# Sparse attention of a two-layer decoder step: scores and values as split fp32r products, a denser compression, probabilities scaled on GpSimd

## The reference, cut to what matters

```python
def compress(k, pe, w):                    # stride 16, blocks of 32 tokens
    ...
    blocks = jnp.concatenate([seg[:, i:i + nc] for i in range(r)], axis=2)
    return jnp.einsum('nclgd,lde->ncge', blocks + pe[:, None, :], w)

def nsa_core(q, q_rot, qpos, ck, cv, fetch, wk, wv, wpos, gates, key_len):
    ...
    p_cmp = jnp.where(cvalid, jax.nn.softmax(jnp.where(cvalid, s, NEG_INF), axis=-1), 0.0)
    o_cmp = jnp.einsum('bghqn,bngd->bqghd', p_cmp.astype(cv.dtype), cv)
    ...
    o = gates[..., 0:1] * o_cmp + gates[..., 1:2] * o_slc + gates[..., 2:3] * o_win
```

## Time and profile before

| what | us |
|---|---|
| runs | 1518.56, 1520.88, 1523.13 |
| median of the runs | 1520.88 |
| profiled execution, span of the core | 1521.6 |
| PE busy | 1469.1 (97%) |
| DVE, POOL, ACT busy | 577.0, 515.6, 484.7 |

### The profile page before, as it was taken

The page is one execution under the profiler, slowest core; times in us unless marked ns, Lnnn a source line. Parts: engine busy times, 40 slices in busy tenths (PEclk is TensorE's granted clock), DMA queues, the critical chain, the costliest instruction groups (busy, mean ns, idle before and its releaser), DMA issues.

```text
span 1521.6 us, 26668 instructions
## 1 busy us (share of the span) xinstructions
PE 1469.1 (97%) x10754; PEld 1322.9 (87%) x10754; DVE 577.0 (38%) x985; ACT 484.7 (32%) x731; POOL 515.6 (34%) x136
## 2 busy tenths in 40 slices
PE   7997999999999999999898999999899999999998
PEld 6997999999999999999584445447799999999997
DVE  5347442222223333143556555552242222223232
ACT  5311342232232333112015556552233222223232
POOL 6422334334336555332201000000233443444652
PEclk9998999999999999999979999999899999999999
DMA  5221222332322333353610000006233223222332
GB/s 188 84 84 56 85 84 83 101 92 83 94 82 77 95 95 111 111 133 120 125 54 22 1 1 1 0 1 184 46 100 95 83 84 109 83 74 82 89 95 76
DMA packets 208062, 124.02 MB, mean 82 GB/s; under 512 B 30964, under 2 KB 205100, under 8 KB 207998
## 3 DMA queue, kind: packets, MB, share of 16 engines
q1 hardware_dynamic: 207998, 123.14, 27.6%
HBM read 117.75 MB, written 5.38 MB: 81 GB/s over the span
## 4 chain that ended last, share of the span: by engine, by line
PE 50%; issue 33%; POOL 10%; SPq 2%; DMA 2%; DVE 1%; ACT 1%; POOLq 0%; DVEq 0%; ACTq 0%
PE PG L430 31%; POOL WL L1632 10%; PE PG L974 5%; PE M L1020 5%; PE M L1008 3%; PE M L947 2%; DMA WBD<-in_w_cmp 1%; PE PG L958 1%; POOL SQX L1627 1%; DMA SLOT<-in_cache_win 1%; PE M L1120 1%; SPq L785 1%; PE M L908 1%; SPq L789 1%; SPq L790 0%
## 5 line engine op out<-in xcount | busy, mean ns | idle before, releaser
L1632 POOL TENSOR_TENSOR WL<-WR,WH 128x2048 fp32r<-128x2048 f32 x105 | 484.6, 4615 | 691.4 <-ACT WH L490 691.4
L430 PE MATMUL PG<-H,WH 128*128 128x260 f32 x4128 | 671.4, 285 | 18.7 <-DVE P L1855 11.0
L430 PEld LDWEIGHTS PG<-H,WH 128*128 128x128 f32 x4128 | 568.4, 190 | 21.3 <-DVE P L1855 11.4
L430 PE MATMUL PG<-H,WL 128*128 128x260 f32 x2064 | 417.5, 283 | 0.0
L430 PEld LDWEIGHTS PG<-H,WL 128*128 128x128 f32 x2064 | 319.7, 189 | 0.0
L430 PE MATMUL PG<-G,WH 128*128 128x260 f32 x1920 | 309.2, 283 | 1.5 <-DVE G L1392 1.5
L490 ACT ACTIVATE WH<-WR 128x2048 fp32r<-128x2048 f32 x105 | 200.4, 1908 | 275.5 <-PE PG L430 243.6
L430 PEld LDWEIGHTS PG<-G,WH 128*128 128x128 f32 x1920 | 263.7, 189 | 1.7 <-issue 1.7
L430 PE MATMUL PG<-G,WL 128*128 128x260 f32 x960 | 194.0, 283 | 0.0
L430 PEld LDWEIGHTS PG<-G,WL 128*128 128x128 f32 x960 | 148.5, 189 | 0.0
L607 DVE TENSOR_TENSOR TB<-PG,RSTD 128x520 f32<-128x520 f32 x44 | 30.8, 699 | 213.0 <-PE PG L430 213.0
(11 more groups left out here) (228 smaller groups left out, 1071.0 us busy)
## 6 DMA issues: line engine op xcount, KB each, us to landing
WR<-in_w_ffn_in SPq DMA_DIRECT2D x88, 512.0 KB, 4.6
WR<-in_w_in SPq DMA_DIRECT2D x32, 512.0 KB, 4.4
WR<-in_w_ffn_out SPq DMA_DIRECT2D x32, 384.0 KB, 3.8
WR<-in_w_ffn_out SPq DMA_DIRECT2D x32, 320.0 KB, 3.2
WR<-in_w_in SPq DMA_DIRECT2D x18, 256.0 KB, 3.5
WR<-in_w_out SPq DMA_DIRECT2D x8, 512.0 KB, 3.8
PST<-in_cache_kv SPq DMA_DIRECT2D x32, 128.0 KB, 2.1
WR<-in_w_out SPq DMA_DIRECT2D x16, 256.0 KB, 5.9
```

The lines of the kernel that those rows point to most:

```text
L430: mm = pe.matmul(PG[:, par, hf, 0:HALF], w, x, start=(first and at_k == 0 and n == 0), stop=(last and at_k == nk - 1 and n == 2))
L1632: w_split.on(pool.tensor_tensor(WL[:, b, :], WR[:, b, :], WH[:, b, :].bitcast(F32), ALU.subtract))
```

## The change

- **Compression.** `CT` holds two tokens of a pair of rows in the two partition halves, so 8 matrices `WC` (128 x 128, two half blocks side by side) replace 32 `WBD`: 8 x 2 products of 320 and 322 columns. Half of the result is then in the other partition half: ACT copies it across (`other_half`) and DVE adds (`drain_ck`). A page is loaded by four DMAs. `WC` is loaded as soon as its slot is free.
- **Queries and keys.** POOL forms the rotated queries in `RT` (cosine product, then sum), ACT writes the high part to `QST`, DVE the low part to the other partition half. Keys get a high part `KA` (ACT) and a low part `KB` (DVE), and SP copies each to the other partition half (`d_dup`). A score is then two fp32r products, and the mask.
- **Values** are split into `VSH` (ACT) and `VSL` (POOL), laid out with zeros between the halves, so that a product writes all 128 partitions. `PT` becomes `PTH` (ACT) and `PTL` (DVE); a key tile is three fp32r products.
- **The loop** runs over 88 tiles (`UNITS`). Probabilities have three buffers, scores come two steps ahead, spread over the tiles of a step (`share`); a reciprocal of four columns on DVE, scaling on POOL.
- **The compressed softmax**: subtraction and final multiplication move from DVE to POOL; the mask after the exponential goes (the maximum is cut off at NEG/10).
- **Order.** Padding of the sample queries, loads of sample keys 1 to 7, of the sample constants and of the first output weights, and the split of the first of these, move behind the loop or its last score.

```diff
+        UNITS = [(hu, kt) for hu, (gp, i, e, br) in enumerate(STEPS)
+                 for kt in ([None] if hu % 4 == 0 else []) + list(range(i + 1))]
...
+            for kv in range(2):
+                for h in range(2):
+                    for b in range(2):
+                        sp.dma_start(WC[h * HD:(h + 1) * HD, kv, :, b, :],
...
+            for n, (gp, e, br) in enumerate(STACKS):
...
+                sp.wait_ge(k_lo.sem, n + 1)
+                for x in (KA, KB):
+                    sp.dma_start(x[other, br, 2 * gp + e, :].bitcast(F32), x[r, br, 2 * gp + e, :].bitcast(F32)
+                                 ).then_inc(d_dup[n], 16)
...
+            sp.wait_ge(v_lo.sem, 1)
+            cache(0, 0, 0)
+            sp.wait_ge(s_done.sem, 4 * len(STEPS))
+            for n in range(1, NS):
                 cache(0, n, 0)
+            sp.dma_start(CS[:, :], a["c_smp"]).then_inc(d_cs, 16)
+            sp.wait_ge(pv_done.sem, len(UNITS))
             for n in range(NS):
                 cache(1, n, 0)
             for n in range(NS):
                 cache(0, n, 1)
-            sp.wait_ge(ss_done.sem, 2)
+            sp.wait_ge(d_kv, 32 * (QT + 1))
+            load_out1(sp, 0)
             for n in range(NS):
                 cache(1, n, 1)
+            load_out1(sp, 1)
...
+            for m in range(KD):
+                if m >= 3:
+                    pool.wait_ge(qst_ok.sem, m - 2)
+                x = RT[:, m % 3, :]
+                rt_cos.on(pool.tensor_tensor(x, P0[:, m, :], COS, ALU.mult))
+                pool.wait_ge(rt_cos.sem, m + 1)
+                pool.wait_ge(rope_in.sem, 4 + m + 1)
+                rt_ok.on(pool.tensor_tensor(x, x, SQ[:, m % 2, :], ALU.add))
...
+            for hu in range(len(STEPS)):
+                if hu < 2:
+                    c_ready.on(pool.tensor_tensor(TC[hu][:, :, :, :], TC[hu][:, :, :, :], spread(hu), ALU.mult))
+                gp, i, e, br = STEPS[hu]
+                pool.wait_ge(rc_ok.sem, hu + 1)
+                for j in range(4):
+                    pj = PB[hu % 3][j][:, 0:(i + 1) * P]
+                    f, g = 32 + 4 * (hu % 4) + j, 3 * (4 * (2 * gp + e) + j) + 1 + br
+                    p_ready.on(pool.tensor_scalar(pj, pj, ST4[:, f:f + 1], GT[:, i, g:g + 1], ALU.mult, ALU.mult))
+            pool.wait_ge(s_done.sem, 4 * len(STEPS))
+            z_q.on(pool.memset(QPD[:, :], 0.0))
...
-                for l in range(32):
+                for r in range(8):
...
+                    for c, n in ((0, 2 * GSEG), (1, 2 * GSEG + 2)):
+                        mm = pe.matmul(M[:, 2 + c, 0:n], WC[:, kv, r, :, :].rearrange("p b e -> p (b e)"),
+                                       CT[:, r, c * 2 * GSEG:c * 2 * GSEG + n], start=r == 0, stop=r == 7)
...
+                pe.matmul(bank[:, 0:n], q, KA[:, br, 2 * gp + e, 0:n], start=True, stop=False)
+                pe.matmul(bank[:, 0:n], q, KB[:, br, 2 * gp + e, 0:n], start=False, stop=False)
...
+                pe.matmul(O, vh, hi, start=kt is None, stop=False)
+                pe.matmul(O, vh, lo, start=False, stop=False)
+                pv_done.on(pe.matmul(O, vl, hi, start=False, stop=last))
...
+            for j in range(4):
+                score(1, j)
+            for x, (hu, kt) in enumerate(UNITS):
+                if hu + 2 < len(STEPS):
+                    for j in share(hu, x - U_0[hu]):
+                        score(hu + 2, j)
+                if x >= 2:
+                    pv(x - 2)
+                turn(x)
...
+            for m in range(KD):
+                if m >= 2:
+                    dve.wait_ge(rt_ok.sem, m - 1)
+                dve.wait_ge(rope_p.sem, 4 + m + 1)
+                rope_in.on(dve.tensor_tensor(halves(SQ[:, m % 2, :]), rope_banks(4 + m), halves(SIN), ALU.mult))
+                if m:
+                    stack_low(m - 1)
...
+            stack_low(KD - 1)
...
+            for n in range(len(STACKS)):
+                key_low(n)
+                if n == 1:
+                    dve.wait_ge(cmp_done.sem, 1)
+                    prompt_ct(dve, 1, 1, ct_v)
             for job in SETUP_V:
                 drain_job(dve, 0, job)
...
+            for x, (hu, kt) in enumerate(UNITS):
+                if hu + 2 < len(STEPS):
+                    for j in share(hu, x - U_0[hu]):
+                        row_max(hu + 2, j)
+                if x == U_0[hu] and hu + 1 < len(STEPS):
+                    recip(hu + 1)
+                low_part(x)
...
+            for x, (hu, kt) in enumerate(UNITS):
+                high_part(act, x)
...
+                if hu + 2 < len(STEPS):
+                    for j in share(hu, x - U_0[hu]):
+                        exp(hu + 2, j)
```

More of the change, by code:

```diff
@@ L344, in program @@
         d_wc = [sem("d_wc_k"), sem("d_wc_v")]
+        d_dup = [sem(f"d_dup{n}") for n in range(8)]
         d_kv, d_gs, d_cs = (sem(n) for n in ("d_kv", "d_gs", "d_cs"))
@@ L654, in program @@
         Q_ATT = Q_CV + 2
[L655 to L662, removed]
+        UNITS = [(hu, kt) for hu, (gp, i, e, br) in enumerate(STEPS)
+                 for kt in ([None] if hu % 4 == 0 else []) + list(range(i + 1))]
+        N_U = [sum(1 for h, _ in UNITS if h == hu) for hu in range(len(STEPS))]
+        U_0 = [sum(N_U[:hu]) for hu in range(len(STEPS) + 1)]
+        Q_SMP = Q_ATT + len(UNITS)
         KV_TILE = (12, 16)
         def by_act(q):
-            return Q_ATT <= q < Q_SMP or q % 2 == 1
+            return q % 2 == 1 and q != Q_CV and not Q_ATT <= q < Q_SMP
         DRAINED = [[by_act(x) for x in range(q + 1)].count(by_act(q)) for q in range(Q_SMP + 2 * NS + 4)]
@@ L1296, in pad_queries @@
                     qpd_ok.on(c)
-            row_max(0)
+            for j in range(4):
+                row_max(0, j)
             drain_ck(1)
-            drain_cv(dve, 0)
-            scale_probs(0)
-            for hu in range(len(STEPS)):
-                if hu % 4 == 0 and hu:
-                    o_low(hu // 4 - 1)
-                if hu + 1 < len(STEPS):
-                    row_max(hu + 1)
-                    if 4 <= hu < 8:
-                        pad_queries(hu - 4)
-                    scale_probs(hu + 1)
+            chain(dve.memset(ACC[:, :], 0.0))
@@ new lines, in dve_attention @@
+            for gp in range(2):
+                dve.wait_ge(c_exp.sem, gp + 1)
+                vec.on(dve.tensor_reduce(CM[gp], TC[gp][:, :, :, :], AX.X, ALU.add))
+            dve.wait_ge(vec.sem, vec.now)
+            chain(dve.tensor_scalar(CM2, CM2, 1e-30, None, ALU.max))
+            chain(dve.reciprocal(CM2, CM2))
+            dve.wait_ge(gt_ok.sem, 1)
+            for gp in range(2):
+                g = GT[:, :, :].rearrange("p i (g j b) -> p i g j b", g=NKV, b=3)[:, :, 2 * gp:2 * gp + 2, :, 0]
+                cm = CM[gp].rearrange("p i (j e) -> p i e j", e=2)
+                c = dve.tensor_tensor(cm, cm, g, ALU.mult)
@@ new lines, in dve_attention @@
+            c_gate.on(c)
+            recip(0)
+            drain_cv(dve)
+            for j in range(4):
+                row_max(1, j)
+            for x, (hu, kt) in enumerate(UNITS):
[5 more added lines that the diff above has]
+                low_part(x)
+                if x - 3 + 1 in O_AT:
+                    o_low(O_AT[x - 3 + 1])
@@ L1322, in own_rows, with high_part @@
+        def high_part(act, x):
+            rows = 2 * NC if UNITS[x][1] is None else P
+            q = Q_ATT + x
+            act.wait_ge(q_fill.sem, q + 1)
+            if x >= 4:
+                act.wait_ge(pv_done.sem, x - 3)
+            pt_hi.on(act.activation(PTH[0:rows, x % 4, :], M[0:rows, q % 2, :], ACT.Copy))
         def own_rows(x):
```

555 lines of the change are left out of this document (292 added, 263 removed).

## The result

| | before | after |
|---|---|---|
| median of the runs, us | 1514.79 (20 runs, 1511.08 to 1523.13) | 1508.18 (20 runs, 1506.21 to 1509.62) |
| ratio | 1 | 0.9944 (95%: 0.993 to 0.9958) |
| profiled execution: span | 1521.6 | 1505.8 (its own time 1507.97) |
| queries projected | 728.1 | 739.1 |
| first transposes of the loop | 805.26 | 837.93 |

Faster, by 0.56% where 2.6% was forecast; 1508 lies at the far end of the range (1450 to 1513). The profiled execution of before is near the upper end of its runs, so the spans lie 15.8 us apart and the medians 6.6. What follows the start of out1 takes 441.2 and 441.4 us.

A forecast was written before the change was run, and what follows sets the result against it. TensorE (PE) alone was taken to bound the loop. Loop -55, ahead of it +11, queues +1 and samples +3 give -40, so 1521 becomes 1481 us, range 1450 to 1513.

The forecast's parts named there:

- the paragraph on queues: SP's DMA issues: further page DMAs +1 us (0 to 3.5); key copies nothing, without cover +2; sample keys nothing, without it +3.
- the 734 us for the compression weights: Ahead of the loop: weights asked for before the queries end, landing near 734, so most of an 11.33 us wait goes.
- the terms ahead of the loop: From rotation through value pages and second compression to loop start near 816.5: +11 us (+2 to +18).
- The loop: Attention over key tiles: cheaper fp32r products shorten it from 223.64 to 169 us, -55; ends 156 and 200.
- i = 0: Loop steps with one key tile: a chain through ScalarE's copies and exponentials, not PE, sets 3.6 us a step.
- GpSimd's scaling: Scaling of probabilities in the loop: 2.3 ns a column, 6.0 us for a step of i = 3, covered, costing nothing.
- Rival 3: In the loop, GpSimd's scaling becomes the bound: at 6 ns a column the kernel takes 1558 us; chance 0.07.
- The rotation: Queries' rotation ahead of the loop: GpSimd and VectorE block each other, 4.0 us a tile, 2.7 if only VectorE waits.
- The samples: After the loop: padding the sample queries costs 3 us, output weights' transfer none: +3 us (0 to 7).
- Rival 2: Loop falls short: VectorE's low part in each tile replaces the passes removed; 1512 to 1522 us; chance 0.17.
- Rival 1: Nothing held up: GpSimd and VectorE do not block each other, loop reaches PE's floor; -65, 1456 us; chance 0.17.
- rival 4: Products no cheaper: fp32r at 512 columns takes two passes, scores stay; 1564 us; chance 0.03.

The follow-up runs named there:

- e3: Changed kernel with SP's sixteen copies of keys issued behind pages 13 to 15 instead of ahead of them: 1498.64 us, ratio 0.9892.
- e5: Changed kernel with query weights ahead of pages, compression weights ahead of pages 11 and 12, key copies behind pages 13 to 15: 1483.59 us, ratio 0.9781.
- e1: Changed kernel with the first slot's query weights asked for ahead of the pages, pages 0 to 4 between the slots: 1497.24 us, ratio 0.9887.
- e11: Changed kernel with the probabilities scaled by VectorE instead of GpSimd: 1528.14 us, ratio 1.0082.
- e10: Changed kernel with the third value product of every key tile left out, so less exact: 1494.06 us, ratio 0.9852.
- e6: As e5, with GpSimd making the cosine products of the first three query tiles early, later ones two tiles ahead: 1482.38 us, ratio 0.9764.
- e8: As e6, with value pages drained between key low parts, and compressed softmax sums and second-step maxima moved ahead on VectorE: 1473.71 us, ratio 0.9721.
- e9: As e8, but the rotation's cosine products made by VectorE instead of GpSimd: 1476.32 us, ratio 0.9733.
- e12: As e8, with the eight sample columns of a rotated tile copied by ScalarE: 1475.28 us, ratio 0.9715.

## Why the prediction was wrong

**The failed step is the paragraph on queues, and the 734 us for the compression weights.** It named two of the three places (pages ahead of the query weights, copies ahead of pages 13 to 15) and priced both near nothing; that the compression weights stand behind pages it did not see:
- "Ten more without reads, at a third of that ... +1 (0 to 3.5)": the twenty took 10.9 us more than the ten, so each of the ten further DMAs cost 1.09 us and not 0.34. PE's last key tiles did not cover it: PE waited 8.3 us, and the queries ended 11.0 us later. The layout was not priced at all: in 256-byte chunks an issue takes 599 ns instead of 342, for the ten that were there before as well.
- "The weights land near 734": I had them asked for as soon as their slot was free, but SP first had to issue the eight page DMAs ahead of them in its program, 7.88 us, and those stood behind the late queries. They landed near 746.7.
- The copies, "nothing, without that cover +2": PE waited 6.6 us for pages, and e3 gave 7.4 us ahead of the loop. I let pages 13 to 15 wait for DVE to free the bank; two of the pages that they replace had been transposed before the rotation ended.

By the terms ahead of the loop, forecast and measured: first sum of the rotation ends near 737 and at 751.0 (**+14.0**); seven more tiles 28 and 25.8 (-2.2); from there to the third page 13.5 and 14.4 (+0.9); the pages to the second compression 14.5 and 23.5 (**+9.0**); from that to the loop 23.5 and 23.3 (-0.2). The two large ones are SP's but for 2.4 us: in e5 the first sum ends at 734.5, and from the third page to the second compression it takes 16.9 us, as a page takes 2.45 us there and not 2.1. The loop then starts at 814.7. Between the two spans the forecast is 24 us off: 20.7 ahead of the loop, 6.8 in it, -3.4 in the samples. The other 9 us, from 15.8 between the spans to 6.6 between the medians, are the spread of the kernel before.

**The loop** was right in mechanism and 6.5 us too short, 169 for 175.5. PE's timeline of one score and one key tile of i = 3, and the next score (start, us):

```profile
989.16 0.47 PE L1057 MATMUL PG<-KA,QST 128*128 128x512 f32 x1
989.48 0.40 PE L1058 MATMUL PG<-KB,QST 128*128 128x512 f32 x1
989.71 0.23 PE L1060 MATMUL PG<-CBF 128*128 128x128 bf16 x1
989.75 0.48 PE L1111 MATMUL M<-PTH,VSH 128*128 128x512 f32 x1
990.07 0.39 PE L1112 MATMUL M<-PTL,VSH 128*128 128x512 f32 x1
990.30 0.39 PE L1113 MATMUL M<-PTH,VSL 128*128 128x512 f32 x1
990.53 0.60 PE L1090 MATMUL M<-BASE,PB 128*128 128x128 f32 x4
990.89 0.47 PE L1057 MATMUL PG<-KA,QST 128*128 128x512 f32 x1
```

By the starts: score 0.32 + 0.23 + 0.04 = 0.59 (0.51 forecast), products 0.32 + 0.23 + 0.23 = 0.78 (0.69), transposes 0.36 (0.59): 1.73 for 1.79. The fp32r price was right for a product behind another and 0.09 low for the first of a kind; the transposes came out cheaper than the earlier trace rows had them. The term that failed is i = 0: its pairs take 20.5 and 18.3 us where 15.7 was forecast, 7.4 us together. Half of that is the clock: in the first 20.5 us it is 0.66, hence mostly the 1.2 GHz level. In e1 and e3 it was 0.92 there, that pair took 16.9 us and the loop 171.7.

**GpSimd's scaling** stayed below the bound that I took:

```profile
L925 POOL TENSOR_SCALAR PB<-PB,ST,GT x128: 450/612/788, 835.2 to 1003.6; 128x128 f32<-128x128 f32 x32, 128x256 f32<-128x256 f32 x32, 128x384 f32<-128x384 f32 x32, 128x512 f32<-128x512 f32 x32
```

That is 0.45 us for 128 columns and 0.78 for 512, where I took 0.63 and 1.50. A further column costs near 0.9 ns, the lower end, and not 2.3. Rival 3 is out by measurement, and e11 shows its mirror image.

**The rotation** at 4.0 us a tile (3.57 measured) was right because both engines wait:

```profile
L897 POOL TENSOR_TENSOR RT<-P,CA x8: 1279/1742/1767, 740.0 to 773.2; 128x520 f32<-128x520 f32 x8
L900 POOL TENSOR_TENSOR RT<-RT,SQ x8: 1280/1789/1796, 749.8 to 775.0; 128x520 f32<-128x520 f32 x8
L1293 DVE TENSOR_TENSOR QST<-RT,QST x16: 684/686/1682, 753.5 to 783.1; 64x512 fp32r<-64x512 f32 x16
```

POOL's sum takes 1.28 us alone and 1.79 beside DVE, DVE's low part 0.69 and 1.68. That agrees with the rule of the Trainium skill that I weighed (SBUF — State Buffer, Who interferes with whom): whoever starts second is blocked until the other's instruction has ended. By it the tile was the 4.0, without it 2.7.

**The samples** (+3, measured -0.4): the padding cost what I took for it, but the transfers, which now run on behind the last score, gave something back for which I took nothing. First line, the kernel after: its first sample product. Second line, the kernel before: the wait that is gone.

```profile
1016.43 1.22 PE L1152 MATMUL PG<-CKT,Q 128*128 128x128 f32 x4 [3.08 <-DVE QPD L1380]
1067.21 8.83 PE L1120 MATMUL M<-SLOT,PTP 128*128 128x256 f32 x32 [2.20 <-DMA SLOT<-in_cache_win]
```

PE waits 3.1 us for the padded queries and no longer 2.2 for the last window values. The first output weights, for which I took nothing, cost nothing: PE has no wait for them.

**Rivals.** Rival 2 gave 1512 to 1522, near the result, for a reason that e10 rules out: no hand-over set the loop. That its number came near is luck: whoever read only the total would have taken it for confirmed. Rival 1 is out, as POOL and DVE do block each other; rival 4, as a product of 512 columns takes 0.23 us behind another. The direction was right, the size nearly five times too large. What I had named as a sign, PE idle ahead of the loop and released by POOL and DVE, was there (DVE 11.5 and 7.0 us), but beside it stood 22.5 us of waits that end with a DMA. Of these I had named only late pages, as the upper end of a term (+18 for +11), and not the two waits for weights.

## What to carry to other kernels

Price a DMA that is added to a queue at a whole issue, from rows of that queue with the same layout, and then list what is asked for behind it in program order: here 32 more page DMAs and sixteen copies held back what stood behind them, which took back half of a gain of 48 us, and moving three blocks of issue code returned it. When a queue is one engine's program, put what the critical engine needs next ahead of what is only prefetched. Read a result by stages, not by its total, or a rival may seem confirmed by a sum to which its own mechanism gave nothing.

## What the runs showed that was not expected

- The issue time of a DMA on SP differed with its layout, at the same number of bytes or fewer: 342 ns for 128 KB in 128 partitions and 1 KB chunks, 477 for half of that in 64 partitions, 599 for 64 KB in 256-byte chunks.
- A small instruction is held up as well: DVE's copy of eight columns takes 0.16 us alone and, beside GpSimd's products, 0.53 in the changed kernel and 0.75 in e6 (medians).
- The same loop took 171.7, 175.5 or 179.5 us in kernels that differ only ahead of it, at a mean granted clock of 0.98, 0.95 or 0.92. What decides which of them a kernel gets was not settled: in the 23.3 us ahead of the loop PE worked for 14.62 us in the changed kernel and for 14.72 in e1, and the clock in the first 20.5 us of the loop was 0.66 and 0.92. The difference is as large as the effect of e8, e9 or e12.
